# The experts' down weights loaded as two neighbouring rows per partition, in one segment of 8 KB

## The reference, cut to what matters

```python
def expert_block(args):
    xb, e = args
    return (jax.nn.silu(xb @ w_gate[e]) * (xb @ w_up[e])) @ w_down[e]
```

## Time and profile before

| | |
|---|---|
| median of 3 runs | 2216.79 us (2215.71 to 2218.95) |
| the profiled execution | 2218.15 us, of which the span from first to last instruction is 2216.3 us |
| mean granted TensorE clock | 0.993 of full speed |
| moved by DMA | 565.44 MB in 214533 packets |
| q1, the queue of SyncE | 210562 packets, 550.39 MB |
| packets under 8 KB | 213762 |
| loads of gate, up, down weights of the experts | 112 each of 1024.0 KB |

### The profile page before, as it was taken

How to read it: one execution, slowest core, us unless ns; L and a number is a source line. 1 busy time by engine, 2 the same in 40 slices (tenths; PEclk the granted TensorE clock), 3 DMA queues, 4 the chain that set the end, 5 groups by cost and what they waited for, 6 DMA issues and landing times.

```text
span 2216.3 us, 26738 instructions
## 1 busy us (share of the span) xinstructions
PE 2142.0 (97%) x10344; PEld 1745.5 (79%) x10344; DVE 1607.5 (73%) x1539; ACT 1333.7 (60%) x1418; POOL 74.8 (3%) x133
## 2 busy tenths in 40 slices
PE   8999999989999999999999999898999999999998
PEld 7787888877888888778877887676678888888887
DVE  5686445875455689999999989999766566576656
ACT  5644444463454577877787778777444446564445
POOL 0001000002400000000000000001010000000000
PEclk9999999999999999999999999999999999999999
DMA  9307556545766799999999999999534655524642
GB/s 324 109 1 242 170 178 211 193 151 199 264 210 234 248 368 377 409 404 410 386 409 405 410 387 410 390 409 387 166 122 139 222 179 201 172 90 149 228 171 77
DMA packets 214533, 565.44 MB, mean 255 GB/s; under 512 B 9990, under 2 KB 47618, under 8 KB 213762
## 3 DMA queue, kind: packets, MB, share of 16 engines
q1 hardware_dynamic: 210562, 550.39, 67.5%
q0 software_dynamic: 3808, 13.27, 1.7%
q10 hardware_dynamic: 32, 0.02, 0.0%
HBM read 548.94 MB, written 14.68 MB: 254 GB/s over the span
## 4 chain that ended last, share of the span: by engine, by line
PE 75%; DVE 13%; DMA 6%; ACT 4%; issue 2%; SPq 0%; DVEq 0%; ACTq 0%
DVE wl L2232 9%; PE up L2838 6%; PE up L2839 6%; PE up L2844 6%; PE acc L3846 5%; DMA raw<-in_moe_w_up 5%; PE acc L3851 3%; PE tp L3813 2%; PE up L3813 2%; ACT wh L1346 2%; PE up L3353 2%; PE acc L3004 2%; PE up L3347 1%; PE acc L3347 1%; PE acc L3414 1%
## 5 line engine op out<-in xcount | busy, mean ns | idle before, releaser
L2232 DVE TENSOR_TENSOR wl<-raw,wh 128x2048 fp32r<-128x2048 f32 x336 | 758.5, 2287 | 142.5 <-ACT wh L1346 140.9
L1346 ACT ACTIVATE wh<-raw 128x2048 fp32r<-128x2048 f32 x336 | 640.9, 1921 | 227.8 <-PE up L3353 41.5
L1903 DVE TENSOR_TENSOR wl<-raw,wh 128x2048 fp32r<-128x2048 f32 x168 | 384.4, 2291 | 271.7 <-ACT wh L1081 270.5
L1081 ACT ACTIVATE wh<-raw 128x2048 fp32r<-128x2048 f32 x168 | 321.8, 1917 | 279.0 <-PE up L2844 103.1
L2838 PE MATMUL up<-wh,xT 128*128 128x512 f32 x608 | 241.4, 397 | 3.6 <-DVEq L2522 1.9
L2839 PE MATMUL up<-wh,xT 128*128 128x512 f32 x608 | 236.6, 390 | 0.0
L2844 PE MATMUL up<-wl,xT 128*128 128x512 f32 x608 | 162.0, 388 | 0.0
L2838 PEld LDWEIGHTS up<-wh,xT 128*128 128x128 f32 x608 | 114.8, 189 | 29.3 <-issue 6.2
L2839 PEld LDWEIGHTS up<-wh,xT 128*128 128x128 f32 x608 | 114.8, 189 | 22.8 <-issue 0.5
L2844 PEld LDWEIGHTS up<-wl,xT 128*128 128x128 f32 x608 | 113.7, 188 | 23.8
L3353 PE MATMUL acc<-wl,xT 128*128 128x512 f32 x336 | 94.9, 405 | 5.3 <-DVE wl L2232 3.7
(11 more groups left out here) (586 smaller groups left out, 3670.3 us busy)
## 6 DMA issues: line engine op xcount, KB each, us to landing
raw<-in_moe_w_gate SPq DMA_DIRECT2D x112, 1024.0 KB, 10.9
raw<-in_moe_w_up SPq DMA_DIRECT2D x112, 1024.0 KB, 10.5
raw<-in_moe_w_down SPq DMA_DIRECT2D x112, 1024.0 KB, 11.7
raw<-in_ffn_w SPq DMA_DIRECT2D x64, 1024.0 KB, 5.6
raw<-in_hg_w_in SPq DMA_DIRECT2D x15, 1024.0 KB, 13.1
raw<-in_da_w_in SPq DMA_DIRECT2D x12, 1024.0 KB, 6.4
raw<-in_ffn_w_gate SPq DMA_DIRECT2D x22, 512.0 KB, 6.2
raw<-in_ffn_w_up SPq DMA_DIRECT2D x22, 512.0 KB, 7.5
```

Of the source, the lines that this page charges most:

```text
L1081: f(wh[:, q % SPLITS, :], raw_half(q), ACT.Copy).then_inc(s_hi, 1)
L1346: f(wh[:, x % SPLITS, :], raw[:, x % RAW, :], ACT.Copy).then_inc(moe["hi"], 1)
L1903: V.tensor_tensor(wl[:, q % SPLITS, :], raw_half(q), wh[:, q % SPLITS, :].bitcast(F32), ALU.subtract).then_inc(s_lo, 1)
L2232: V.tensor_tensor(wl[:, x % SPLITS, :], raw[:, x % RAW, :], wh[:, x % SPLITS, :].bitcast(F32), ALU.subtract).then_inc(moe["lo"], 1)
```

## The change

The down weights are laid out by another function: partition p gets rows 2 p and 2 p + 1 of the 256, which are neighbours in HBM. The load's access pattern becomes 128 runs of 2048 floats on both sides, so 8 KB each, where it was 256 runs of 1024. It holds for all 126 such loads in the program (14 of the first expert, 98 of the seven visits, 14 in the loop over further visits, which the inputs here do not enter). Slot, bytes, waits and place in SyncE's order stay.

Since block k of a unit must now hold the channels 2 c + k (c from 0 to 127, within each 256), the six instructions that bring gate and up sums to SBUF write in that order: they read 512 neighbouring floats as before, and of two neighbours the second goes 128 floats (512 bytes) further on. Their output pattern is 2 x 128 x 2 with the innermost step 128. The turns, the products and all other instructions stay as they are, and no instruction is added, removed or moved on any engine.

```diff
+    def pairs_apart(a):
+
+        return a.rearrange("p (h k c) -> p h c k", k=2, c=P)
+
+    def pairs_together(a):
+
+        return a.rearrange("p (h c k) -> p h c k", k=2, c=P)
...
+        row_pairs = lambda w: w.rearrange("(p k) n -> p k n", p=P)
+
-        def load_half(at, t_, p, w, k, cols_, n, waits=True):
+        def load_half(at, t_, p, w, k, cols_, n, waits=True, form=kp):
...
-            ld(raw[:, x % RAW, :].rearrange("p (k n) -> p k n", k=n), kp(w[k:k + n * P, cols_]), m_ready[x % RAW])
+            ld(raw[:, x % RAW, :].rearrange("p (k n) -> p k n", k=n), form(w[k:k + n * P, cols_]), m_ready[x % RAW])
...
-                load_half(at, *place_of(r + j), w, u * W + j * HALF, slice(0, D), 2)
+                load_half(at, *place_of(r + j), w, u * W + j * HALF, slice(0, D), 2, form=row_pairs)
...
-            f(stage[:, u % 2, :], acc[:, 2 + u % 2, :], ACT.Copy).then_inc(moe["st"], 1)
+            f(pairs_apart(stage[:, u % 2, :]), pairs_together(acc[:, 2 + u % 2, :]), ACT.Copy).then_inc(moe["st"], 1)
...
-            f(own_ups, up[:, 1, :], ACT.Copy).then_inc(own["act"], 1)
+            f(pairs_apart(own_ups), pairs_together(up[:, 1, :]), ACT.Copy).then_inc(own["act"], 1)
...
-            V.tensor_tensor(stage[:, u % 2, :], light_gates[1 if u == EU - 1 else u % 2], acc[:, 2 + u % 2, :], ALU.mult).then_inc(moe["st"], 1)
+            V.tensor_tensor(pairs_apart(stage[:, u % 2, :]), pairs_together(light_gates[1 if u == EU - 1 else u % 2]),
+                            pairs_together(acc[:, 2 + u % 2, :]), ALU.mult).then_inc(moe["st"], 1)
```

More of the change, by code:

```diff
@@ L739, in load_down @@
             for part in (1, 0) if u == 0 else (0, 1):
-                load_half(at, t_, p + part, w, u * W + part * HALF, slice(0, D), 2, waits=u > 0 or part == 1)
+                load_half(at, t_, p + part, w, u * W + part * HALF, slice(0, D), 2, waits=u > 0 or part == 1, form=row_pairs)
         def heavy_rows(memory, n):
@@ L1376, in light_gate @@
             act.wait_ge(moe["T"], at(EU, u // 2 * 2))
-            f(light_gates[1 if u == EU - 1 else u % 2], up[:, u % 2, :], ACT.Copy).then_inc(moe["act"], 1)
+            f(pairs_apart(light_gates[1 if u == EU - 1 else u % 2]), pairs_together(up[:, u % 2, :]), ACT.Copy).then_inc(moe["act"], 1)
         def wide_silu(at, u):
@@ L1411, in own_gate @@
             wait_count(act, own["turned"], own_from["turned"] + 2 * u - 1)
-            f(own_gates, up[:, 0, :], ACT.Copy).then_inc(own["act"], 1)
+            f(pairs_apart(own_gates), pairs_together(up[:, 0, :]), ACT.Copy).then_inc(own["act"], 1)
         def own_up(u):
@@ L2266, in gate_times_up @@
             dve.wait_ge(moe["up"], at(EU, t_ + 1))
-            V.tensor_tensor(stage[:, 0, :], half[:, 0, :], up[:, 1, :], ALU.mult).then_inc(moe["st"], 1)
+            V.tensor_tensor(pairs_apart(stage[:, 0, :]), pairs_together(half[:, 0, :]), pairs_together(up[:, 1, :]), ALU.mult).then_inc(moe["st"], 1)
         def light_half(at, r):
```

## The result

| | |
|---|---|
| kernel before | median 2217.28 us (2213.83 to 2219.45, 15 runs) |
| changed kernel | median 2221.69 us (2217.26 to 2224.41, 15 runs) |
| ratio | 1.0021, 95% interval 1.0014 to 1.0028 |

Single executions of one kernel lie up to 7 us apart.

A forecast was written before the change was run, and what follows sets the result against it. The prediction took TensorE as the bound before 880 us and the DMA queue after. Loads gain 4.2 + 0.2 = 4.4 us, copies cost nothing: 2216.8 - 4.4 = 2212.4 us, range 2209.6 to 2217.4.

The forecast's parts named there:

- Packets: Down loads: 128 packets fewer for each of the 112 that run, 196,226 left in q1; 0.05 us saved per load.
- I take f = 1: Six copy and product lines: writes 512 bytes apart cost the same per element as neighbouring ones, factor f = 1, 0 us.
- the formula: First expert and first heavy visit: 7 x 0.445 (f - 1) + 7 x (0.445 (f - 1) - 0.35, if positive) + 2 x 0.536 (f - 1).
- its two cases: Far writes in the six lines: f about 2, 4.9 us, chance 0.12; f of 3 or more, 12.1 us, chance 0.08.
- Each shortens a queue that never empties: After 880 us: every down load's saving counts, in light and heavy visits alike, 84 x 0.05 = 4.2 us.
- The rival in which light visits alone gain: Visits: TensorE sets the heavy ones, so only four light visits count, 56 x 0.05 = 2.8 us, 2214.0 us; chance 0.12.
- the 4.2 us of 84 loads: Six visits after 880 us: 14 down loads each, gaining 0.05 us per load, 4.2 us in all.
- more per packet: Down loads of all visits, first heavy one included: 98 x 0.07 = 6.9 us gained, 2209.9 us; chance 0.13.
- stays above 7 us: Loads before the second light visit: their landing time would remain over 7 us, against 7.9 us in the kernel before.
- the experts end 4 us earlier: End of the experts: their last load would land about 4 us earlier.
- The rival at f = 2: First expert and first heavy visit: copies cost 4.9 us against 4.4 gained by loads, 2217.3 us; chance 0.12.
- its partner, 4.4 us from the loads: Down loads: 4.2 us after 880 us and 0.2 us from the first heavy visit, 4.4 us gained.

The follow-up runs named there:

- the one that reads apart: 8 KB loads as in the changed kernel, but the six instructions read every second float and write neighbours; against the kernel before 0.9984, again 0.999.

## Why the prediction was wrong, step by step

**Packets: right.** Counts to the packet, and 315 ns for an 8 KB packet where 316.4 was read off the two loads of ple_rows. By rates a load saves 0.05 to 0.07 us. The fixed 3 cycles per packet of the Trainium skill ("DMA: Bandwidth & Descriptors", section "Why small descriptors are slow (HBM only)") made an estimate of 0.03, which is too little here.

**"I take f = 1": wrong, and it turned the sign.** The step argued from an even pace per element of writes that were all of neighbours. No such row can tell what a jump costs. The factor is 2.1 to 2.2 on ScalarE and 1.8 on VectorE. For the first expert the formula itself held: with the measured growth it is 7 x 0.49 + 7 x (0.49 - 0.35) = 4.4 us, the traces show 0.64 us per unit and 4.05 in six, and the kernel with far writes there alone lost 6.0 us (3.3 to 8.4). Its last term, 2 x 0.42 at the first heavy visit, makes 5.3 in all; the wait there grew by 0.72. It left out that the first turns of the other two heavy visits wait 0.7 us longer as well. What reaches the total of that isn't told: all seven visits together lost 2.0 us (-0.2 to 4.2). The section "SBUF Cachelines" of "Advanced Engine Details and Errata" in the Trainium skill had named the effect. The runs agree with its line of 16 bytes, for writes (nearly nothing at 8 bytes, all at 16, no more at 512), and it should have had more than 0.20 between its two cases.

**"Each shortens a queue that never empties": half wrong.** The queue is the bound of the light visits only, as far as the traces tell. A heavy visit is TensorE's, at 111.3 to 111.4 us with loads of 2, 4 and 8 KB, and its loads' saving ends in a queue that runs nearly empty. The rival in which light visits alone gain, with the measured price, gives 56 x 0.05 to 0.07, 2.8 to 3.9 us; the kernel with 8 KB loads alone gained 2.7, the one that reads apart 3.5 and 2.2. These intervals don't exclude the 4.2 us of 84 loads by themselves; the steps between the turns, the landing times and the gaps of the DMA engines do speak for the rival. The 6.9 us of "more per packet" lie outside all three intervals. That the queue before the second light visit "stays above 7 us" was a test that I had set, and it failed at 5.2. It was a weak one, as two kernels that load in 4 KB runs but write far in the visits show 6.2 and 6.3 there. Nor did the experts end 4 us earlier: counted from the first expert's first turn, TensorE's work right behind the last visit (L2794 of before) starts at 976.14 us in place of 971.84.

**The sum.** -2.7 from the loads and +6.4 from the copies make +3.7, measured +4.7 (3.1 to 6.2). The rival at f = 2 had the mechanism of the copies right, with its 4.9 us, and its partner, 4.4 us from the loads, was too large: with 2.7 it would have been 2219.0.

**Open.** How much of its own 14 x 0.06 = 0.8 us a light visit really gains isn't settled: 0.5 in the pair of traces above, some 0.65 by the means, and differences of that size are those between two executions. Nor is a landing time a sure gauge of the queue: at the end of the first heavy visit (loads issued from 869 to 879 us) the kernel with 8 KB loads and plain copies has 7.5 us at a DMA share of 0.89, where before has 5.5 at 1.00.

## What to carry to other kernels

A layout that makes a load cheaper has to be paid for where the data is put in the matching order: let the read side of a copy out of PSUM jump, not the write side, above all where TensorE waits for the copy. A pattern that no row shows has no price yet, so rows of neighbouring writes should leave both signs open. A full queue does not make its engines the bound: look where its landing times are shortest, and whether its engines have gaps there. A saving counts only as far as that reserve goes; the loss here counted nearly in full.

## What the runs showed of the hardware

- A copy of 512 floats per partition from PSUM to SBUF costs 0.49 to 0.55 us more on ScalarE, and a product 0.40 to 0.43 us more on VectorE, when successive writes are 16 bytes or more apart (1.09 to 1.14 us in place of 0.59 or 0.60, and 1.08 to 1.11 in place of 0.68); steps of 8 bytes cost ScalarE 0.04 us. At 32 bytes it was 1.20 on ScalarE, and at 512 and 1024 bytes no more than at 16.
- Reads from PSUM at 16, 512 or 1024 bytes apart cost ScalarE nothing (580 to 598 ns).
- A weight load in steps of two floats took 206 ns in place of 141, and 219 in place of 155, in turns of 128 rows; in those of 64 it took 196 in place of 191 or 192.
- 1 MB loads in packets of 2, 4 and 8 KB move 389, 410 and 418 to 422 GB/s with a full queue.
